# Ten norms: roots with tokens on partitions, spread back by TensorE

## What is computed

```
def rms_norm(x, g):
    xf = x.astype(jnp.float32)
    y = xf * lax.rsqrt(jnp.mean(xf * xf, axis=-1, keepdims=True) + NORM_EPS)
    return (y * g.astype(jnp.float32)).astype(x.dtype)

def layernorm(x, g, b):
    mean = jnp.mean(x32, axis=-1, keepdims=True)
    var = jnp.mean(jnp.square(x32 - mean), axis=-1, keepdims=True)
    y = (x32 - mean) * lax.rsqrt(var + LN_EPS)
```

## Time and profile before

| | |
|---|---|
| median of 3 runs | 4427.17 us (4422.57 to 4432.58) |
| profiled execution | 4413.36 us |
| its span | 4411.6 us |
| mean granted TensorE clock | 0.951 |
| PE busy | 3869.1 us (88%) |
| DVE busy | 2044.8 us (46%) |
| ACT busy | 944.1 us (21%) |
| POOL busy | 715.1 us (16%) |

### The profile page before, as it was taken

The page is one execution under the profiler, slowest core; times in us unless marked ns, Lnnn a source line. Parts: engine busy times, 40 slices in busy tenths (PEclk is TensorE's granted clock), DMA queues, the critical chain, the costliest instruction groups (busy, mean ns, idle before and its releaser), DMA issues. The chain is left out here.

```text
span 4411.6 us, 79392 instructions
## 1 busy us (share of the span) xinstructions
PE 3869.1 (88%) x35448; PEld 2544.8 (58%) x35448; DVE 2044.8 (46%) x3165; ACT 944.1 (21%) x1649; POOL 715.1 (16%) x571
## 2 busy tenths in 40 slices
PE   5999999969999989787999677777788999999986
PEld 2458885435788845454555567667654555554432
DVE  2537723355684249924100244555423444541593
ACT  2411100000110020011002333334212444441101
POOL 0024441000444400000001432223000000000000
PEclk8999999989999989898997699999999999999998
DMA  1123323422332112102222211111101111111120
GB/s 59 53 78 137 106 90 124 180 96 105 130 137 81 63 57 67 38 23 88 93 87 116 88 40 44 36 40 33 74 16 50 53 55 43 48 62 45 60 86 19
DMA packets 113255, 320.38 MB, mean 73 GB/s; under 512 B 8033, under 2 KB 75617, under 8 KB 101153
## 3 DMA queue, kind: packets, MB, share of 16 engines
q1 hardware_dynamic: 104592, 280.87, 18.4%
q0 software_dynamic: 8336, 34.61, 2.2%
HBM read 278.75 MB, written 30.41 MB: 70 GB/s over the span
## 5 line engine op out<-in xcount | busy, mean ns | idle before, releaser
L724 PE MATMUL lin_ps<-hn,ring 128*128 128x512 f32 (+1 forms) x4448 | 1488.5, 492 | 103.8 <-DVE hn L2016 31.8
L724 PEld LDWEIGHTS lin_ps<-hn,ring 128*128 128x128 f32 x4448 | 848.0, 192 | 701.1 <-issue 623.2
L724 PE MATMUL lin_ps<-arena,ring 128*128 128x256 f32 (+3 forms) x3184 | 1017.9, 486 | 38.7 <-DVE arena L2346 24.8
L724 PEld LDWEIGHTS lin_ps<-arena,ring 128*128 128x128 f32 (+2 forms) x3184 | 615.3, 196 | 417.1 <-issue 328.1
L724 PE MATMUL lin_ps<-arena 64*64 64x64 f32 (+3 forms) x10112 | 559.5, 242 | 110.4 <-issue 51.5
L1506 ACT ACTIVATE arena<-lin_ps 128x512 f32<-128x512 f32 (+4 forms) x463 | 273.9, 608 | 1373.1 <-PE lin_ps L724 1372.2
L724 PEld LDWEIGHTS lin_ps<-arena 64*64 64x64 f32 (+1 forms) x10112 | 429.6, 142 | 194.7 <-issue 121.7
L2016 DVE SCALAR_TENSOR_TENSOR arena<-arena,vec 128x512 f32<-128x512 f32 (+2 forms) x563 | 436.5, 851 | 149.3 <-PE lin_ps L724 148.0
L724 PE MATMUL sum_ps<-arena 64*64 64x64 f32 x7136 | 302.8, 223 | 48.9 <-issue 39.0
L2016 DVE SCALAR_TENSOR_TENSOR arena<-arena,cs 128x512 f32<-128x512 f32 x336 | 335.7, 1067 | 0.0
L724 PEld LDWEIGHTS sum_ps<-arena 64*64 64x64 f32 x7136 | 257.7, 137 | 58.5 <-issue 44.8
(11 more groups left out here) (206 smaller groups left out, 3645.2 us busy)
## 6 DMA issues: line engine op xcount, KB each, us to landing
ring<-w_up SPq DMA_DIRECT2D x32, 1024.0 KB, 6.0
ring<-w_down SPq DMA_DIRECT2D x32, 1024.0 KB, 5.2
arena<-w_mod SPq DMA_DIRECT2D x24, 1024.0 KB, 7.9
arena<-w_mod SPq DMA_DIRECT2D x12, 2048.0 KB, 7.9
features<-arena POOLq DMA_DIRECT2D x64, 384.0 KB, 2.6
ring<-w_attn SPq DMA_DIRECT2D x16, 1536.0 KB, 6.3
ring<-w_conv_in SPq DMA_DIRECT2D x16, 1024.0 KB, 5.8
ring<-features SPq DMA_DIRECT2D x40, 384.0 KB, 3.5
```

The costliest lines, as they stand in the source:

```text
L724: return pe.matmul(out, lhsT, rhs, start=start, stop=stop)
```

## The change

For ten norms the sums are taken with the operands exchanged: each 128x128 block of squares is the weight, and one column of ones streams, so that the sums come with tokens on partitions, 4 or 6 columns of them (`token_sums`). Root and reciprocal work on 128x4 or 128x6 (`std_col`, `inv_col` in `small`). Then each column, broadcast to 128x128 as a weight, is multiplied with the identity, which puts the values of 128 tokens in a row on every partition (`root_rows`), in the columns of `sum_ps` where the sums stood. VectorE multiplies with that row straight from PSUM. ffn0 and ffn1 keep the old form and only their semaphore counts change. The mean inside the convolutions keeps the old form.

```diff
+        ROOTS = {n: i for i, n in enumerate(["mla", "sgu", "first", "c0", "cell0", "rw", "at", "c1", "cell1", "last"])}
+        std_col, inv_col = small[:, 8:8 + KB], small[:, 16:16 + KB]
+        def root_row(c0, cw):
+            return sum_ps[:, 256 + c0:256 + c0 + cw]
...
+            def token_sums(v, width, first, last):
+                for b in range(width // P):
+                    m = mm(sum_ps[:, b:b + 1], v[:, b * P:(b + 1) * P], ones[:, 0:1], first and b == 0, last and b == width // P - 1)
+                if last:
+                    m.then_inc(col_mm, 1)
+            def root_rows(nrm, width):
+                pe.wait_ge(col_inv, ROOTS[nrm] + 1)
+                for b in range(width // P):
+                    m = mm(root_row(ALL - width + b * P, P), inv_col[:, b:b + 1].to_broadcast([P, P]), ident, True, True)
+                m.then_inc(root_mm, 1)
+            def root_sums(nrm, width, src=hn):
+                i = NI[nrm]
+                for k in [0, KD - 1] if nrm in PARTS else range(KD):
+                    pe.wait_ge(sq_ready, 8 * i + k + 1)
+                    if nrm in PARTS and k == 0:
+                        pe.wait_ge(part_sum, PARTS.index(nrm) + 1)
+                    token_sums(last_cols(src[:, k, :], width), width, k == 0, k == KD - 1)
+                root_rows(nrm, width)
...
@@ late_sums (sgu, first)
-                mm(sum_ps[:, 512:1024], ones, late_square(0), True, False)
-                mm(sum_ps[:, 512:1024], ones, late_square(KD - 1), False, True).then_inc(sum_mm, 1)
+                token_sums(late_square(0), SEQ, True, False)
+                token_sums(late_square(KD - 1), SEQ, False, True)
+                root_rows(nrm, SEQ)
...
@@ conv, after the mean
-                            m = mm(sum_ps[:, 256 + c0:256 + c0 + cw], ones, (cy, hn)[part][:, k, c0:c0 + cw], k == 0, k == KD - 1)
-                    m.then_inc(conv_s, 1)
+                for k in range(KD):
+                    pe.wait_ge(conv_sq, 8 * i + k + 1)
+                    token_sums(last_cols(hn[:, k, :], width), width, k == 0, k == KD - 1)
+                root_rows(f"cell{i}", width)
...
@@ scalar
-                act.wait_ge(sum_mm, NI[nrm] + 1)
-                f(last_cols(std, width), sum_ps[:, 1024 - width:1024], ACT.Sqrt, bias=scal(0), scale=1.0 / D).then_inc(std_ready, 1)
+                n = width // P
+                act.wait_ge(col_mm, ROOTS[nrm] + 1)
+                f(std_col[:, 0:n], sum_ps[:, 0:n], ACT.Sqrt, bias=scal(eps), scale=1.0 / D).then_inc(col_std, 1)
...
@@ vector
+            def inverse_root(nrm, width):
+                n = width // P
+                dve.wait_ge(col_std, ROOTS[nrm] + 1)
+                nc.vector.reciprocal(inv_col[:, 0:n], std_col[:, 0:n]).then_inc(col_inv, 1)
+                dve.wait_ge(root_mm, ROOTS[nrm] + 1)
...
-                rd(width, std_ready, NI[nrm] + 1)
+                inverse_root(nrm, width)
...
-                        m = nc.vector.scalar_tensor_tensor(dst(k, c0, cw), xs[:, k, c0:c0 + cw], gain(k, c0), rstd[:, c0:c0 + cw],
+                        m = nc.vector.scalar_tensor_tensor(dst(k, c0, cw), xs[:, k, c0:c0 + cw], gain(k, c0), root_row(c0, cw),
...
-                    stt(c_, c_, V("conv_ln_g_2", 8 * i + k), last_cols(rstd, width), ALU.mult, ALU.mult).then_inc(conv_l, 1)
+                    stt(c_, c_, V("conv_ln_g_2", 8 * i + k), root_row(ALL - width, width), ALU.mult, ALU.mult).then_inc(conv_l, 1)
```

More of the change, by code:

```diff
@@ L331, in build @@
         std_ready = sem("std_ready")
+        col_mm, col_std, col_inv, root_mm = sem("col_mm"), sem("col_std"), sem("col_inv"), sem("root_mm")
         h_ready = sem("h_ready")
@@ L778, in norm_sums @@
                 m.then_inc(sum_mm, 1)
-            norm_sums("mla", SEQ)
+            root_sums("mla", SEQ)
             s = S["dkv"]
@@ L1001, in conv @@
             def conv(i, nrm, width):
-                norm_sums(nrm, width)
+                root_sums(nrm, width)
                 linear(f"conv{i}_ab", KD, 256, full_h, width, wait=(h_ready, 8 * (NI[nrm] + 1)))
                 linear(f"conv{i}_g", KD, 512, full_h, width, wait=(h_ready, 8 * (NI[nrm] + 1)))
[L1006 to L1009, removed]
-                            m = mm(sum_ps[:, 256 + c0:256 + c0 + cw], ones, (cy, hn)[part][:, k, c0:c0 + cw], k == 0, k == KD - 1)
-                    m.then_inc(conv_s, 1)
+                for k in range(KD):
+                    pe.wait_ge(conv_y, 8 * i + k + 1)
+                    for c0, cw in SEGS[width]:
+                        m = mm(sum_ps[:, 256 + c0:256 + c0 + cw], ones, cy[:, k, c0:c0 + cw], k == 0, k == KD - 1)
+                m.then_inc(conv_s, 1)
+                for k in range(KD):
+                    pe.wait_ge(conv_sq, 8 * i + k + 1)
+                    token_sums(last_cols(hn[:, k, :], width), width, k == 0, k == KD - 1)
+                root_rows(f"cell{i}", width)
                 linear(f"conv{i}_out", KD, 512, lambda k, c0, cw: cy[:, k, c0:c0 + cw], width, wait=(conv_out, 8 * (i + 1)))
             conv(0, "c0", ALL)
-            norm_sums("rw", ALL)
+            root_sums("rw", ALL)
             for m_, (name, _) in enumerate(LERPS[:4]):
@@ L1370, in _ @@
             linear("rw_out", KD, 512, full_h, ALL, wait=(y_done, KD))
-            norm_sums("at", ALL, full_cols(atsq))
+            root_sums("at", ALL, atsq)
             s = S["attn"]
@@ L1495, in _ @@
             conv(1, "c1", SEQ)
-            norm_sums("last", SEQ)
+            root_sums("last", SEQ)
         @block.scalar
@@ L1516, in squares, with root @@
                     f(last_cols(dst[:, k, :], width), last_cols(xs[:, k, :], width), ACT.Square).then_inc(sq_ready, 1)
-            def root(nrm, width):
-                act.wait_ge(sum_mm, NI[nrm] + 1)
-                f(last_cols(std, width), sum_ps[:, 1024 - width:1024], ACT.Sqrt, bias=scal(0), scale=1.0 / D).then_inc(std_ready, 1)
+            def root(nrm, width, eps=0):
+                n = width // P
+                act.wait_ge(col_mm, ROOTS[nrm] + 1)
+                f(std_col[:, 0:n], sum_ps[:, 0:n], ACT.Sqrt, bias=scal(eps), scale=1.0 / D).then_inc(col_std, 1)
             def takes_over(name):
@@ L1629, in ffn @@
                     if p == 5:
-                        act.wait_ge(sum_mm, NI[nrm] + 1)
+                        act.wait_ge(sum_mm, i + 1)
                         f(last_cols(std, SEQ), sum_ps[:, 512:1024], ACT.Identity, bias=scal(0), scale=1.0 / D).then_inc(std_ready, 1)
@@ L1683, in conv @@
                     f(last_cols(cg[:, k, :], width), lt(s.buf(k), width), ACT.Silu).then_inc(lin_ev, 1)
-                act.wait_ge(conv_s, 2 * i + 1)
+                act.wait_ge(conv_s, i + 1)
                 f(last_cols(cmean, width), sum_ps[:, 1024 - width:1024], ACT.Copy, scale=1.0 / D).then_inc(conv_n, 1)
@@ L1688, in conv @@
                     f(last_cols(hn[:, k, :], width), last_cols(cy[:, k, :], width), ACT.Square).then_inc(conv_sq, 1)
-                act.wait_ge(conv_s, 2 * i + 2)
-                f(last_cols(std, width), sum_ps[:, 1024 - width:1024], ACT.Sqrt, bias=scal(1), scale=1.0 / D).then_inc(conv_n, 1)
+                root(f"cell{i}", width, 1)
                 for k in range(KD):
@@ L2219, in ffn @@
                     block_sums(down_b[c])
-                rd(SEQ, std_ready, NI[nrm] + 1)
+                rd(SEQ, std_ready, i + 1)
                 by = last_cols(rstd, SEQ).rearrange("p (a b) -> p a b", a=2)
@@ L2334, in conv @@
                     o.wait()
-                dve.wait_ge(conv_n, 2 * i + 1)
+                dve.wait_ge(conv_n, i + 1)
                 for k in range(KD):
@@ L2338, in conv @@
                                             ALU.subtract).then_inc(conv_c, 1)
-                rd(width, conv_n, 2 * i + 2)
+                inverse_root(f"cell{i}", width)
                 for k in range(KD):
                     c_ = last_cols(cy[:, k, :], width)
-                    stt(c_, c_, V("conv_ln_g_2", 8 * i + k), last_cols(rstd, width), ALU.mult, ALU.mult).then_inc(conv_l, 1)
+                    stt(c_, c_, V("conv_ln_g_2", 8 * i + k), root_row(ALL - width, width), ALU.mult, ALU.mult).then_inc(conv_l, 1)
                 for k in range(KD):
```

## The result

The changed kernel takes 4436.67 us (median of 17 runs, 4431.47 to 4443.49), the kernel before 4429.07 us beside it (17 runs, 4422.42 to 4437.90). The ratio is 1.0019, 95% interval 1.0012 to 1.0027, so 8.4 us more, between 5.3 and 12. (A ratio here is taken over all the runs of both kernels; the two medians lie 7.6 us apart.) The forecast was +6.6 us. The measured 0.19% is just inside the 0.2% that the forecast called no change, and the interval reaches beyond it; that the changed kernel is slower is clear of the noise. The profiled execution of the changed kernel took 4441.0 us.

The account below looks back on a forecast made before the run. TensorE, busy 88% of the span, bounds the kernel; norms matter only where it stands still for them. Sums +28.0 and chains -21.4 us, net +6.6 on the median 4427.2, gave 4433.8 us, range 4396 to 4440.

Parts of the forecast that it names:

- The chain: Ten norms, root to first multiplication: 4.11 us becomes 1.80 or 2.43 (512 tokens), 6.00 becomes 2.38 or 3.33 (768).
- The fixed part: Between root and first multiplication, outside the spreading products: 0.59 + 0.05 us at either clock.
- The spread: Products putting the reciprocals in rows: 8 take 1.16 us (high clock) or 1.79 (low), 12 take 1.74 or 2.69.
- PSUM as an operand: First multiplication of each norm now reads PSUM: no cost taken, 0.67 us each at 128x512.
- The sums: One-column products before the root, 0.115 us each (high clock) or 0.224 (low); together +28.0 us over the ten norms.
- the deciding choice: Clock in the long sums of mla, c0 and cell0: stays low, costing +4.63, +8.14 and +9.42 us.
- cell1: cell1's sum: first 16 products at the high clock, 48 at the low, 12.59 us against 7.13, +5.46.
- the second rival: Low clock also in rw, at, c1, last and from cell1's start: 4439.8 us, slower by 0.28%; chance 0.12.
- The short sums: sgu +0.55 us, first -0.17; rw and at 1.38 us, c1 and last 0.92, these four at no cost.
- The first rival: Clock rises in the long sums as today: 27 to 32 us faster, at the middle 4398 us; chance 0.30.
- The sum: Whole kernel, likeliest case: sums +28.0 us, chains -21.4, net +6.6, 4433.8 us.

Follow-up runs that it names:

- e4: Changed kernel with eight extra 512-column products ahead of c0's sums; single execution 4423.46 us, c0's sum 15.62 us in place of 20.64.
- e2: Changed kernel with sgu, first, rw, at, c1 and last back in the old form; 4441.73 us, ratio 1.0039 to the kernel before.
- e1: Changed kernel with mla, c0, cell0 and cell1 back in the old form; 4417.53 us, ratio 0.9983 to the kernel before.
- e5: Changed kernel with cell0 and cell1 old, VectorE adding mla's and c0's eight groups of squares into one; 4411.63 us, ratio 0.9975 to the kernel before.
- e6: Changed kernel with mla, c0, cell0, cell1 old, VectorE adding mla's and c0's squares into one group; 4421.50 us, ratio 0.9987 to the kernel before.
- e7: e5 with cell0 new too, its squares added into one group by VectorE and GpSimd; 4417.15 us, ratio 0.9976 to the kernel before.

## Why the prediction was right, step by step

**The chain.** Forecast 2.43 us (512, low clock), measured 2.64; high clock 1.80 against 1.72 (last). At 768 forecast 3.33, measured 3.51 to 3.58; at rw, where the clock fell during the spread, 2.71. The fixed part was right (root 0.26, reciprocal 0.18, first spread product 0.53 behind the root in c1). The spread was under-sized at the low clock: 2.08 and 2.93 us for 8 and 12, where 1.79 and 2.69 had been taken from a row of products with two columns, while a spread streams 128. Gains of 1.5 and 2.4 us in place of 1.7 and 2.7.

**PSUM as an operand.** 5.36 us for eight, 5.39 before: no cost, as taken.

**The sums.** Pace at the low clock 0.215 us, forecast 0.224; 13.79, 20.64 and 20.55 us for mla, c0 and cell0, forecast 14.34 and 21.50. The low clock was the deciding choice and it held, in each of them, to the last product (in mla by the pace, as said above). e4, in one execution, shows it as a property of these products and not of the place. One reading of the prediction was wrong, without harm to the sum: the all-ones weights did not stand still. The old sum of c0 has 32 weight loads for its 32 products, 0.19 us each at the high clock and 0.34 at the low, hidden under the columns that stream. The exchange does not bring the loads in; it makes them 96 there, and takes away what hid them.

**cell1** was the one choice between far ends: 16 products high, then low. After the change it ran at the low clock from the start (13.81 us, that part of the second rival), in e2 high and then low as forecast (12.18, forecast 12.59). Both occur. What the forecast missed is that the old form depends on the same luck: 13.39 us in the profile it was read from, 15.1 to 16.3 in six others, so the true loss at cell1 is nearer 2.5 than 5.2.

**The short sums.** rw and at 1.50 us at the high clock, forecast 1.38 and no cost; c1 and last 1.05, hidden by the table load, as said. sgu and first cost nothing (2.90 and 3.54 us against 3.03 and 3.75). The rest of the second rival, a clock that has fallen before the last block group, did not come. The timeline and the window of rw's sum after:

```profile
2000.08 1.50 PE L732 MATMUL sum_ps<-con,hn 128*128 128x1 f32 x12 [0.88 <-ACT hn L1542]
```
```profile
2000.10:2001.58 1.48, 1.48 (x12) 1.39 (x12) 0.00 (x0) 1.23 (x1) 0.00 (x0) 1.00 0.95 387
```

**The first rival** (the clock rises, 27 to 32 us faster) fell with the windows above. The Trainium skill (TensorE: Matmul & The Clock Gate, Part 1: The HAM clock gate) says that a busy PE releases the throttle. Taken at its word that would have made this rival the forecast; the windows of c0, cell0 and cell1 above disagree with it for one-column products.

**The sum.** The forecast was +28.0 us of sums and -21.4 of chains, +6.6 net. The profiles of before and after give +26.0 and -20.1, +5.9 net: both terms were a little too large, and the misses cancel. Against the second profile of before the net is +3.1, because the old cell1 was lucky in the first. The ratio says +8.4 (5.3 to 12). So the mechanism and the terms were right, but that 6.6 lies so near 8.4 is in part luck: between 2.5 and 5.3 us of the measured loss are not in the norms, and no term of the prediction stands for them.

That gap stays open. Each ratio is good to some 4 us only, but the sign is the same each time. In every kernel the time is worse than the norms' table says: by 3 to 6 us in e1, 5 to 8 in e5, 6 to 9 in e6 (its norms take 104.1 us), 5 to 8 in e7 (100.9), and by 0 to 3 in e2, the only one that keeps the short norms old. The recurrent stage points the same way: 1336.9, 1337.3 and 1340.9 us in the three profiles with the old rw and at, 1339.1 to 1356.7 in the seven with the new ones. A rival that no run tests is that a shorter norm in front makes the stage behind it longer; seven profiles against three, which overlap, do not show it. Nor does the granted clock account for it, as far as two windows of that stage show, the kernel before and e7:

```profile
1992.42:3329.33 1336.91, 1081.84 (x25988) 830.23 (x25988) 463.31 (x1018) 357.32 (x676) 248.62 (x185) 0.93 0.17 61
```
```profile
1982.55:3337.25 1354.70, 1081.67 (x25996) 830.65 (x25996) 459.52 (x1018) 358.07 (x676) 248.93 (x185) 0.93 0.17 61
```

The mean clock is 0.93 in both and TensorE is busy the same 1082 us; the 17.8 us between them are time in which TensorE stands idle, 273.0 in place of 255.1. What it waits for more was not followed up.

## What to carry to other kernels

Exchanging operands to shrink an elementwise step trades columns streamed for weights loaded. Count the loads on the path: at one block group it is free (2.72 us against 2.92) and the small root and reciprocal are a clear gain; at eight groups the sum takes 1.4 to 1.9 times what the old streams did, since a long run of one-column products stayed at the low clock, or fell to it, however busy it kept TensorE. Cut the groups first, on an engine that is idle there, and not on VectorE and GpSimd at once (e7). Read what one profile says of a stage against a second profile wherever the granted clock changes inside it, and read the clock against the pace of the products.

## What was not expected of the hardware

The granted clock fell from 1.00 to 0.50 in the middle of an unbroken run of products (e4): 4.7 us at 100% busy ran at 1.00, the next 10 us at 100% busy at 0.50. And a weight load of 128 columns is not a fixed time: it took 0.19 us at the high clock and 0.34 at the low in the old sum of c0, and a one-column product took 0.112 and 0.213 in e4. Two f32 adds side by side on VectorE and GpSimd took 2.37 us in place of 0.96 and 2.33 in place of 1.80, because they took turns.
